# Sums of the later modulations on ScalarE and GpSimd in a two-block transformer kernel

## The chip, the cores and the metric

The kernel runs on one core of one Trainium2 chip. The metric is the device time of one execution in microseconds (us), from the core's first instruction to its last. The core has a TensorE (PE in the profile), a VectorE (DVE), a ScalarE (ACT), a GpSimd (POOL) and a SyncE (SP). SP and POOL issue most of the transfers, ACT some of them.

## The reference

Two blocks of a transformer follow each other: a first block with two layers and a second with one, over 512 tokens of width 2048, all in float32. The part that the change touches is the modulation, a product of one vector with a large matrix, once per layer:

```
c_act = jax.nn.silu(c)
mod = c_act @ w_ada[l] + b_ada[l]          # 2048 x 6144 weights per layer
shift, scale, gate = jnp.split(mod, 3, axis=-1)
h = rms_norm(x, norm_g[l]) * (1.0 + scale[:, None, :]) + shift[:, None, :]
...
x = x + gate[:, None, :] * (... @ w_out[l])
```

Everything else (input products, a state space mixer, differential attention, a gated delta rule, sliding window attention, output products) is the same before and after.

## The kernel before

All five engines walk one list of steps, `plan`. Each engine has a function per kind of step, takes the steps that it has a function for, in the order of the list, and skips the others. So the order of instructions on each engine is fixed when the program is built, and semaphores alone join the engines. TensorE's big products are the main line of the list; other generators are interleaved with it, a step at a time.

The weights of the modulations are 128 rows by 512 columns at a time: `modulation(m)` handles one set of blocks of 512 columns, and for each block it runs over 16 row tiles (`KT`), k = 0 to 15. For each k there is a step `ada_sum` and, one yield later, a step `ada_fetch` for the tile three places on. `ada_fetch` is a transfer that GpSimd issues, into one of three slots (in `side` for m = 1 to 4; two in `gring` and one in `const_two` for m = 5). `ada_sum` adds the row tile, times the silu of c of its 128 rows (one column of `cact`), to an accumulator of 128 x 512 in `tring`. It is one VectorE instruction on line 123 (line 120 for k = 0, which has nothing to add to yet), and it frees the slot. When a block's 16 tiles are summed, TensorE's `ada_turn` multiplies the accumulator with a column of ones, which sums over the 128 partitions and puts the result on partitions. It stands at k = 5 of the next block, and `ada_out` adds the bias later.

The first modulation (shift and scale of the first layer) is done by `first_sum` and `first_row` in the first 150 us and is left alone. The five later ones make 448 sums: 384 with weights in `side`, from 184 to 2355 us, and 64 with weights in `gring` and `const_two`, from 3513 to 3820 us. They are served by `carry()`, which runs `carried[0]` of their steps per step of the main line.

Near them on GpSimd stand the steps `powers`, `angles`, `bc_place` and `lags` of the state space mixer, and `rotate` of the attention, which adds two tiles of `tring` into `q` or `k` (the end of the rotary embedding); VectorE makes both tiles just before. On ScalarE stand copies out of PSUM, the exponentials of the softmax and the state space mixer's copies.

The helpers that record the instructions have one line each: 108 matmul, 111 transpose, 114 activation, 117 tensor_tensor, 120 tensor_scalar, 123 scalar_tensor_tensor, 126 tensor_copy, 132 reciprocal, 138 reduce_max, 147 dma_start. So the profile's rows are told apart by their tiles.

Of the kernel before, what the change touches and what calls it, by code (L numbers as in the profile page):

```python
# [18 lines left out]
KT = D // P  # L19
# [242 lines left out]
def build(nc, d, out, at, ncols):  # L262
    ctx = ExitStack()
    with ctx:
# [3 lines left out]
        def sem(name, owner=None):  # L268
            s = Signal(ctx.enter_context(nc.semaphore(name)), owner)
            signals.append(s)  # L270
            return s
# [144 lines left out]
        wide_clear = sem("wide_c_cleared", pool)  # L416
        a_step = sem("act_step", act)
        x_ready_a = sem("x_ready_by_act", act)
# [213 lines left out]
        def ada_slots(m):  # L632
            return wide_slots if m == GATE_OF[2] else mslots
# [782 lines left out]
        def ada_landed(m, n0, k):  # L1416
            return (late_ada_in if m == GATE_OF[2] else ada_in)[ada_slots(m).where["ada", m, n0, k]]
# [28 lines left out]
        def tensor():  # L1446
# [80 lines left out]
            def ada_turn(m, n0):  # L1527
                acc, bank = temps.at("acc", m, n0), aux.at("mod", m)
                if n0 == mods[m][1][0] * D:
                    room(aux.clear("mod", m))  # L1530
                pe.wait_ge(*ada_ready.of("sum", m, n0))
                for j in range(4):
                    c = n0 // P + j
                    i = pe.matmul(bank[:, c:c + 1], acc[:, j * P:(j + 1) * P], ones[:, 0:1], start=True, stop=True)
                i.then_inc(*ada_turned.up(m, n0))
                temps.leave(("acc", m, n0), pe.mine())
# [368 lines left out]
        def vector():  # L1905
# [150 lines left out]

            def ada_sum(m, n0, k):
                acc, wv, c = temps.at("acc", m, n0), ada_slots(m).at("ada", m, n0, k)[:, 0, :], cact[:, mods[m][0] // 2, k:k + 1]
                dve.wait_ge(*ada_landed(m, n0, k).of("ada", m, n0, k))
                if k == 0:  # L2060
                    room(temps.clear("acc", m, n0))
                    i = dve.tensor_scalar(acc, wv, c, None, M)
                else:
                    own()
                    i = dve.scalar_tensor_tensor(acc, wv, c, acc, M, AD)
                i.then_inc(*(ada_ready.up("sum", m, n0) if k == KT - 1 else d_step.up()))
                ada_slots(m).leave(("ada", m, n0, k), dve.mine())
# [668 lines left out]
            def o_turn(j, k0):  # L2736
                if j % 2 == 0:
# [7 lines left out]
                         norm_roots=norm_roots, final_root=final_root, norm_scale=norm_scale, norm_final=norm_final, prm_turn=prm_turn, rope=rope, ada_sum=ada_sum, ada_out=ada_out, norm_square=norm_square, norm_root=norm_root,  # L2745
# [16 lines left out]
        def scalar():  # L2762
# [41 lines left out]
            def late_fetch():  # L2804
# [14 lines left out]
                par(relb[0:32, :], d["rel_bias_2"])  # L2819

# [372 lines left out]
            steps = dict(save_v2=save_v2, set_by=set_by_, rope=rope, norm_square=norm_square, norm_root=norm_root, x_store=x_store, norm_shift=norm_shift, norm_roots=norm_roots, final_root=final_root,  # L3193
# [13 lines left out]
        def gpsimd():  # L3207
# [8 lines left out]
            def ada_fetch(m, n0, k):  # L3216
                w = d["w_ada_2"][0] if mods[m][0] == 2 else d["w_ada"][mods[m][0]]
                room(passed("delta" if m == GATE_OF[2] else "start"))
                room(ada_slots(m).clear("ada", m, n0, k))
                pool.dma_start(ada_slots(m).at("ada", m, n0, k)[:, 0, :], w[k * P:(k + 1) * P, n0:n0 + 512]).then_inc(  # L3220
                    *ada_landed(m, n0, k).landing("ada", m, n0, k))

# [133 lines left out]
            steps = dict(vec_fetch=vec_fetch, ada_fetch=ada_fetch, powers=powers, angles=angles, bc_place=bc_place, lags=lags, rotate=rotate, band=band_,  # L3356
# [129 lines left out]
```

## Time and profile before

| | before |
|---|---|
| time, median of 3 runs | 4302.54 us (4299.52 to 4306.98) |
| the profiled execution: span | 4304.2 us |
| PE busy | 4128.5 us, 96% |
| DVE busy | 2440.3 us, 57% |
| ACT busy | 807.5 us, 19% |
| POOL busy | 498.5 us, 12% |
| chain that ended last: PE, DVE, ACT, DMA | 82%, 12%, 2%, 2% |

The profiled execution's own time is its span, 4304.2 us; the program lays nothing around it that the profile shows. It is 1.7 us over the median of the three runs. Busy time is the time in which an engine runs an instruction. The chain that ended last is followed back from the last instruction, at each step to what released it.

### The profile page before, as it was taken

To read this page: it belongs to the slowest core of one execution; us is meant where nothing else is said; L and a number is where in the kernel's file an instruction comes from. 1 tells how busy PE (TensorE), PEld (TensorE's weight loads), DVE (VectorE), ACT (ScalarE), POOL (GpSimd) and SP (SyncE) were. 2 spreads that over 40 slices of the span, in tenths; PEclk is the share of its full clock that TensorE was granted. 3 is DMA by queue.
4 is the path that set the end of the run, shared out by engine and by line. 5 is a ranking of instruction groups with operands and counts; after the bars stand their busy time and mean duration, and the time that the engine had idled before them with its cause. 6 is when DMAs were issued, how large, how long until landed. Compare 5 with 4: busy or idle time off the path is not lost.

```text
span 4304.2 us, 41305 instructions
## 1 busy us (share of the span) xinstructions
PE 4128.5 (96%) x16042; PEld 2766.0 (64%) x16042; DVE 2440.3 (57%) x4211; ACT 807.5 (19%) x1450; POOL 498.5 (12%) x816
## 2 busy tenths in 40 slices
PE   6899999999999999999999999999999999999999
PEld 3565544444447555444468568878788877787888
DVE  6576436674533564366666466465655367666643
ACT  2222201131011221011311122121211122230000
POOL 0233111111202231111111000000000101100000
PEclk7999999999999999999999999999999999999999
DMA  9633333334552333332444332222121333434433
GB/s 311 204 118 105 108 122 108 121 124 146 151 166 73 105 113 115 121 121 93 130 142 152 113 102 70 64 69 64 61 73 59 92 104 115 126 98 137 137 103 103
DMA packets 370192, 499.29 MB, mean 116 GB/s; under 512 B 44379, under 2 KB 279118, under 8 KB 369486
## 3 DMA queue, kind: packets, MB, share of 16 engines
q1 hardware_dynamic: 289984, 340.16, 24.5%
q0 software_dynamic: 38608, 125.86, 9.2%
q10 hardware_dynamic: 41406, 30.63, 2.2%
q8 instruction: 127, 2.08, 0.2%
q14 instruction: 67, 0.55, 0.0%
HBM read 462.51 MB, written 34.08 MB: 115 GB/s over the span
## 4 chain that ended last, share of the span: by engine, by line
PE 82%; DVE 12%; ACT 2%; DMA 2%; issue 1%; ACTq 0%; POOL 0%; DVEq 0%; SPq 0%
PE bank L108 80%; DVE tring L132 2%; DVE tring L117 2%; PE bank L111 2%; DVE tring L123 2%; DMA side<-in_w_ada 1%; ACT tring L114 1%; DVE wring L117 1%; DVE dring L120 1%; DVE bank L117 1%; DVE tring L120 1%; DVE dring L117 0%; ACT L114 0%; DVE region_b L117 0%; DVE sring L138 0%
## 5 line engine op out<-in xcount | busy, mean ns | idle before, releaser
L108 PE MATMUL bank<-region_b,wring 128*128 128x256 f32 (+2 forms) x4448 | 1322.8, 451 | 7.8 <-ACT region_b L114 6.6
L108 PE MATMUL bank<-region_a,wring 128*128 128x256 f32 (+1 forms) x3232 | 1083.5, 489 | 29.1 <-DVE wring L117 29.1
L108 PEld LDWEIGHTS bank<-region_b,wring 128*128 128x128 f32 (+1 forms) x4448 | 830.2, 190 | 412.5 <-issue 332.3
L108 PEld LDWEIGHTS bank<-region_a,wring 128*128 128x128 f32 x3232 | 613.8, 194 | 416.2 <-issue 337.8
L147 POOL DMA_DIRECT2D side<-in_w_ada x384 | 209.0, 545 | 1309.9 <-DVE tring L123 951.7
L123 DVE SCALAR_TENSOR_TENSOR tring<-side,cact,tring 128x512 f32<-128x512 f32 x360 | 303.2, 842 | 78.1 <-DMA side<-in_w_ada 42.3
L108 PE MATMUL bank<-wring,region_b 128*128 128x512 f32 (+1 forms) x640 | 265.5, 572 | 10.7 <-ACT region_b L114 10.7
L114 ACT ACT_TABLE_LOAD x160 | 205.3, 1283 | 354.2 <-DVE sring L120 283.8
L117 DVE TENSOR_TENSOR tring<-bank,tring 128x256 f32<-128x256 f32 (+1 forms) x229 | 101.0, 441 | 299.6 <-PE bank L108 296.2
L117 DVE TENSOR_TENSOR wring<-wring 128x1024 f32<-128x1024 f32 (+1 forms) x213 | 234.8, 1102 | 17.4 <-PE bank L108 8.5
L108 PE MATMUL bank<-wring,region_a 128*128 128x512 f32 x512 | 226.8, 601 | 6.0 <-ACT region_a L114 6.0
L114 ACT ACTIVATE tring<-bank 128x512 f32<-128x512 f32 (+1 forms) x166 | 81.4, 493 | 796.5 <-PE bank L108 476.2
L108 PEld LDWEIGHTS bank<-wring,region_b 128*128 128x128 f32 x640 | 150.4, 239 | 118.8 <-issue 89.9
L117 DVE TENSOR_TENSOR tring<-bank,side 32x512 f32<-32x512 f32 (+1 forms) x160 | 110.0, 687 | 163.5 <-PE bank L108 159.5
L108 PEld LDWEIGHTS bank<-wring,region_a 128*128 128x128 f32 x512 | 126.6, 250 | 98.1 <-issue 68.7
L132 DVE RECIPROCAL tring<-tring 128x512 f32<-128x512 f32 x54 | 180.7, 3346 | 15.0 <-ACT tring L114 15.0
L108 PE MATMUL bank<-yaT,wring 128*128 128x512 f32 (+1 forms) x512 | 170.6, 486 | 0.0
L117 DVE TENSOR_TENSOR bank<-bank,tring 128x256 f32<-128x256 f32 (+1 forms) x213 | 110.2, 517 | 84.2 <-PE bank L108 81.7
L117 DVE TENSOR_TENSOR tring<-tring 128x512 f32<-128x512 f32 (+2 forms) x142 | 98.7, 695 | 81.6 <-ACT tring L114 77.2
L108 PEld LDWEIGHTS bank<-yaT,wring 128*128 128x128 f32 x512 | 97.1, 190 | 66.9 <-issue 60.3
L114 ACT ACTIVATE tring<-bank,sring 128x128 f32<-128x128 f32 (+3 forms) x128 | 67.2, 526 | 386.7 <-DVE sring L120 386.5
L111 PE MATMUL bank<-const,tring 128*128 128x128 f32 (+1 forms) x474 | 78.8, 282 | 42.9 <-DVE tring L120 13.0
(285 smaller groups left out, 4320.6 us busy)
## 6 DMA issues: line engine op xcount, KB each, us to landing
wring<-in_w_in SPq DMA_DIRECT2D x180, 1024.0 KB, 5.3
side<-in_w_ada POOLq DMA_DIRECT2D x384, 256.0 KB, 3.2
wring<-in_w_out SPq DMA_DIRECT2D x48, 1024.0 KB, 8.2
yaT<-in_w_ada SPq DMA_DIRECT2D x16, 1024.0 KB, 9.4
wring<-in_w_glu SPq DMA_DIRECT2D x16, 1024.0 KB, 7.7
tring<-x_saved SPq DMA_DIRECT2D x48, 256.0 KB, 2.9
gring<-in_w_ada POOLq DMA_DIRECT2D x43, 256.0 KB, 3.0
SS<-in_w_ada SPq DMA_DIRECT2D x8, 1024.0 KB, 9.8
```

Source lines behind the costliest of these rows:

```text
L108: return self.e.matmul(*a, **k) if self.e else self
L111: return self.e.transpose(*a) if self.e else self
L114: return self.e.activation(*a, **k) if self.e else self
L117: return self.e.tensor_tensor(*a) if self.e else self
L120: return self.e.tensor_scalar(*a) if self.e else self
L123: return self.e.scalar_tensor_tensor(out=o, in0=a, scalar=s, in1=b, op0=op0, op1=op1) if self.e else self
L132: return self.e.reciprocal(*a) if self.e else self
L147: return self.e.dma_start(dst, src, allow_slow_non_contiguous=True) if self.e else self
```

## The change

`ada_sum` leaves VectorE. ScalarE waits for the landing of the tile and scales it by the column of `cact` with a Copy activation, in place in its slot (for k = 0 straight into the accumulator, which frees the slot). GpSimd waits for that, and adds the slot to the accumulator with a tensor_tensor (for k = 1 to 15), which frees the slot. TensorE's `ada_turn` now waits for the last addition. The list of steps is the same.

```diff
@@ tensor, ada_turn
-                pe.wait_ge(*ada_ready.of("sum", m, n0))
+                pe.wait_ge(*rows_added.of(m, n0, KT - 1))
@@ vector
-            def ada_sum(m, n0, k):
-                acc, wv, c = temps.at("acc", m, n0), ada_slots(m).at("ada", m, n0, k)[:, 0, :], cact[:, mods[m][0] // 2, k:k + 1]
-                dve.wait_ge(*ada_landed(m, n0, k).of("ada", m, n0, k))
-                if k == 0:
-                    room(temps.clear("acc", m, n0))
-                    i = dve.tensor_scalar(acc, wv, c, None, M)
-                else:
-                    own()
-                    i = dve.scalar_tensor_tensor(acc, wv, c, acc, M, AD)
-                i.then_inc(*(ada_ready.up("sum", m, n0) if k == KT - 1 else d_step.up()))
-                ada_slots(m).leave(("ada", m, n0, k), dve.mine())
@@ scalar
+            def ada_sum(m, n0, k):
+                w = ada_slots(m).at("ada", m, n0, k)[:, 0, :]
+                act.wait_ge(*ada_landed(m, n0, k).of("ada", m, n0, k))
+                if k == 0:
+                    room(temps.clear("acc", m, n0))
+                act.activation(w if k else temps.at("acc", m, n0), w, ACT.Copy, scale=cact[:, mods[m][0] // 2, k:k + 1]).then_inc(
+                    *rows_scaled.up(m, n0, k))
+                if k == 0:
+                    ada_slots(m).leave(("ada", m, n0, k), act.mine())
@@ gpsimd
+            def ada_sum(m, n0, k):
+                if k == 0:
+                    return
+                acc = temps.at("acc", m, n0)
+                pool.wait_ge(*rows_scaled.of(m, n0, k))
+                own()
+                pool.tensor_tensor(acc, acc, ada_slots(m).at("ada", m, n0, k)[:, 0, :], AD).then_inc(*rows_added.up(m, n0, k))
+                ada_slots(m).leave(("ada", m, n0, k), pool.mine())
```

The order of TensorE's and SyncE's instructions is the same in both programs. On VectorE rows go away and none moves against another. These are the rows where VectorE goes from the rotary embedding of a head (`tring<-bank,side`) to the softmax of the one before (`sring`, `tring<-tring,sring,small`), in the first attention:

```order
 L138 TENSOR_REDUCE sring<-bank 128x1
 L120 TENSOR_SCALAR sring<-sring 128x1
-L123 SCALAR_TENSOR_TENSOR tring<-side,cact,tring 128x512 x3
 L117 TENSOR_TENSOR tring<-bank,side 128x512
 L117 TENSOR_TENSOR tring<-bank,side 32x512 x4
```

Three sums that stood ahead of a head's rotary products are gone, and the same holds ahead of the reciprocals of the softmax.

GpSimd in the same place, from the last step of the first state space mixer to the first two `rotate`, before:

```order
164 L117 TENSOR_TENSOR Tm<-const,prm 128x512
165 L147 DMA side<-in_w_ada 128x512 x5
166 L117 TENSOR_TENSOR q<-tring 128x512
167 L147 DMA side<-in_w_ada 128x512 x3
168 L117 TENSOR_TENSOR q<-tring 128x512
169 L147 DMA side<-in_w_ada 128x512 x4
170 L117 TENSOR_TENSOR k<-tring 128x512
```

and now:

```order
236 L147 DMA side<-in_w_ada 128x512
237 L117 TENSOR_TENSOR tring<-tring,side 128x512
238 L117 TENSOR_TENSOR q<-tring 128x512
239 L147 DMA side<-in_w_ada 128x512
240 L117 TENSOR_TENSOR tring<-tring,side 128x512
241 L147 DMA side<-in_w_ada 128x512
242 L117 TENSOR_TENSOR tring<-tring,side 128x512
243 L147 DMA side<-in_w_ada 128x512
244 L117 TENSOR_TENSOR tring<-tring,side 128x512
245 L117 TENSOR_TENSOR q<-tring 128x512
```

Each fetch has an addition ahead of it, and a `rotate` stands with an addition before it and another, after one fetch, behind it.

ScalarE a little later, between the exponentials of the softmax (`tring,sring<-bank,sring`) and the copies of its transposed weights (`wT<-bank`), before:

```order
234 L114 ACTIVATE tring,sring<-bank,sring 128x128 x2
235 L114 ACTIVATE wT<-bank 128x4x128
236 L114 ACTIVATE tring,sring<-bank,sring 128x256 x2
237 L114 ACTIVATE tring<-tring 128x512
238 L114 ACTIVATE wT<-bank 128x128
```

and now:

```order
300 L114 ACTIVATE tring,sring<-bank,sring 128x128 x2
301 L114 ACTIVATE side<-side,cact 128x512
302 L114 ACTIVATE wT<-bank 128x4x128
303 L114 ACTIVATE side<-side,cact 128x512
304 L114 ACTIVATE tring,sring<-bank,sring 128x256 x2
305 L114 ACTIVATE tring<-tring 128x512
306 L114 ACTIVATE side<-side,cact 128x512
307 L114 ACTIVATE wT<-bank 128x128
```

A scaling, with its wait for a landing, stands between the exponentials and the copies. The loads of activation tables (160) are as many as before and none is added.

## Rows read from the trace of the kernel before

**Rows 1.** Busy time by stretches in which modulations are summed, and their sum

```profile
core 0: us, PE busy (x) PEld busy (x) DVE busy (x) ACT busy (x) POOL busy (x), PEclk, DMA share, GB/s
...
1680.00:2100.00 420.00, 408.74 (x1086) 182.96 (x1085) 229.11 (x429) 68.01 (x149) 61.93 (x93) 0.99 0.34 110
...
sum 2516.00, PE 2453.61 PEld 1391.77 DVE 1449.87 ACT 529.73 POOL 446.00; mean PE 350.51 PEld 198.82 DVE 207.12 ACT 75.68 POOL 63.71
```

**Rows 2.** TensorE's waits from 174 to 2360: total us, times, longest

```profile
PE bank L111 <- DVE tring L123: 12.6, 11, 2.3
PE bank L108 <- ACT tring L114: 11.0, 5, 2.8
PE bank L108 <- ACT region_a L114: 6.0, 1, 6.0
...
PE bank L108 <- POOL k L117: 2.6, 2, 1.3
```

**Rows 3.** Pieces of the chain that ended last: start, length, what

```profile
904.41 1.79 DVE tring L123
...
906.38 0.42 DVE tring L120
...
915.75 0.76 DVE tring L123
...
916.60 0.75 DVE tring L123
...
925.50 0.75 DVE tring L123
...
927.00 0.76 DVE tring L123
...
3771.18 0.76 DVE tring L123
```

**Rows 4.** VectorE's sums: duration in ns, min/median/max, first and last start

```profile
L123 DVE SCALAR_TENSOR_TENSOR tring<-side,cact,tring x360: 750/752/1846, 188.5 to 2353.8; 128x512 f32<-128x512 f32 x180
...
L123 DVE SCALAR_TENSOR_TENSOR tring<-gring,cact,tring x40: 750/752/753, 3516.0 to 3818.4; 128x512 f32<-128x512 f32 x40
```

**Rows 5.** The tile `side`: its users, and who waited for its landings

```profile
L120 DVE TENSOR_SCALAR tring<-side,cact x24: 459/481/750, 184.3 to 2296.4; 128x512 f32<-128x512 f32 x24
...
  DVE tring L123: 42.3, 23
```

**Rows 6.** Timeline from 784 to 800: start, us, instruction, idle before it

```profile
788.87 3.56 DVE L117 TENSOR_TENSOR tring<-bank,side 128x512 f32<-128x512 f32 x5 [3.64 <-PE bank L108]
792.52 1.26 POOL L117 TENSOR_TENSOR q<-tring 128x512 f32<-128x512 f32 x1 [7.31 <-DVE tring L117]
792.54 1.79 DVE L123 SCALAR_TENSOR_TENSOR tring<-side,cact,tring 128x512 f32<-128x512 f32 x1
...
794.50 0.35 DVE L120 TENSOR_SCALAR tring<-tring,sring,small 128x128 f32<-128x128 f32 x1
```

**Rows 7.** Timeline from 349 to 352: VectorE reads PSUM beside GpSimd

```profile
349.02 2.31 DVE L123 SCALAR_TENSOR_TENSOR Tm<-bank,const_one,Tm 128x512 f32<-128x512 f32 x4 [1.25 <-PE bank L108]
349.34 0.30 POOL L117 TENSOR_TENSOR W<-cf,Bn 128x64 f32<-128x64 f32 x1
```

**Rows 8.** GpSimd's operations on line 117: duration in ns, min/median/max

```profile
L117 POOL TENSOR_TENSOR q<-tring x16: 1256/1259/1803, 533.8 to 2044.1; 128x512 f32<-128x512 f32 x16
```

**Rows 9.** GpSimd's fetches into `side`: durations, and time to landing

```profile
L147 POOL DMA_DIRECT2D side<-in_w_ada x384: 537/537/804, 174.3 to 2346.9; - x192
...
DMA to landing us min/median/max: 2.8/3.2/8.4
```

**Rows 10.** ScalarE's groups by form: busy us, mean ns, idle before

```profile
L114 ACT ACTIVATE tring<-tring 128x512 f32<-128x512 f32 x91 | 55.4, 626 | 254.9 <-DVE tring L120 189.6 <-DVE tring L123 46.3 <-DVE tring L126 18.1
...
L114 ACT ACTIVATE tring<-region_a,vec 128x512 f32<-128x512 f32 x16 | 11.3, 707 | 0.0
```

**Rows 11.** GpSimd's waits over the whole span: total us, times, longest

```profile
POOL side L147 <- DVE tring L123: 951.7, 239, 64.9
```

More of the change, by code:

```diff
@@ L416, in build @@
         wide_clear = sem("wide_c_cleared", pool)
+        rows_added = sem("ada_rows_added", pool)
         a_step = sem("act_step", act)
+        rows_scaled = sem("ada_rows_scaled", act)
         x_ready_a = sem("x_ready_by_act", act)
@@ L2744, in vector @@
             steps = dict(vec_turn=vec_turn, w_sum=w_sum, fold=fold, quarter_sums=quarter_sums, quarter_rest=quarter_rest, quarter_last=quarter_last, x_turn=x_turn, first_sum=first_sum, first_out=first_out, sum_square=sum_square,
-                         norm_roots=norm_roots, final_root=final_root, norm_scale=norm_scale, norm_final=norm_final, prm_turn=prm_turn, rope=rope, ada_sum=ada_sum, ada_out=ada_out, norm_square=norm_square, norm_root=norm_root,
+                         norm_roots=norm_roots, final_root=final_root, norm_scale=norm_scale, norm_final=norm_final, prm_turn=prm_turn, rope=rope, ada_out=ada_out, norm_square=norm_square, norm_root=norm_root,
                          keep_u=keep_u, c_turn=c_turn, ssm_params=ssm_params, c_power=c_power,
@@ L3191, in o_turn @@
                     aux.leave(("o_turn", j, k0), act.mine())
-            steps = dict(save_v2=save_v2, set_by=set_by_, rope=rope, norm_square=norm_square, norm_root=norm_root, x_store=x_store, norm_shift=norm_shift, norm_roots=norm_roots, final_root=final_root,
+            steps = dict(ada_sum=ada_sum, save_v2=save_v2, set_by=set_by_, rope=rope, norm_square=norm_square, norm_root=norm_root, x_store=x_store, norm_shift=norm_shift, norm_roots=norm_roots, final_root=final_root,
                          vec_fetch=vec_fetch, vec_turn=vec_turn, x_turn=x_turn, first_keep=first_keep, sum_square=sum_square,
@@ L3354, in band_fetch @@
                         *band_in.landing())
-            steps = dict(vec_fetch=vec_fetch, ada_fetch=ada_fetch, powers=powers, angles=angles, bc_place=bc_place, lags=lags, rotate=rotate, band=band_,
+            steps = dict(vec_fetch=vec_fetch, ada_fetch=ada_fetch, ada_sum=ada_sum, powers=powers, angles=angles, bc_place=bc_place, lags=lags, rotate=rotate, band=band_,
                          d_qd=d_qd, oa_store=oa_store, oa_fetch=oa_fetch, v_fetch=v_fetch, band_fetch=band_fetch, fence=fence_of(pool))
```

## The prediction

> **What bounds the kernel now.** I read the page's busy shares first: PE 96%, DVE 57%, ACT 19%, POOL 12%. TensorE is the bound, so a lighter VectorE is worth only what TensorE idles for it. Next I read the stretches in which modulations are summed (174 to 2360 and 3500 to 3830) [rows 1]: 2516 us in all, of which TensorE is busy 2453.6. So it idles 62.4 us there, 2.5%, and no arrangement of the sums can give more than that. VectorE is busy 1449.9 of those 2516 us, ScalarE 529.7, GpSimd 446.0: there is room on both new engines. Then TensorE's own waits [rows 2]: 12.6 us for an operation of VectorE's line 123, 11.0 for ScalarE (exponentials that come after VectorE), 2.6 for GpSimd's `rotate` into `k`. A single 6.0 is the norm of the second layer, which no sum stands in; the rest is spread thin.
>
> Last I walked the chain that ended last for sums of the later modulations. There are 39 pieces, the first at 792.54, the last at 3771.18, 30.4 us together [rows 3, 6]. Most are 0.75 long, five are 1.78 to 1.84 [rows 3, 4]. In the first state space mixer (174 to 500) there is none.
>
> **What is removed.** 420 fused operations at 0.752 us median, 0.842 mean where `side` is the source, and 28 scalings at 0.48 [rows 4, 5]: about 303 + 45 + 13 = 361 us of VectorE. Off the path that is worth nothing. On the path I set each TensorE wait against the sums on the chain just ahead of it, and took the smaller of the two, since TensorE cannot gain more than it waits. Over some two dozen waits this makes 20.9 us. (At 927.90, for one, TensorE had waited 0.66 us, and the chain has 0.76 + 0.75 + 0.75 of sums before it [rows 3], so 0.66 count.)
>
> **The long sums.** The sum at 792.54 took 1.79 us, not 0.75, and ended when GpSimd's `rotate` (792.52, 1.26 us) was through plus one normal duration [rows 6]. The row shows that a VectorE operation with both tiles in SBUF stands still while GpSimd reads SBUF. At 349.02 four VectorE operations that read PSUM took 2.31 us together beside GpSimd's 128x64 products, their normal time [rows 7]. The reverse is seen too: `rotate` took 1.80 at most, 1.26 in the median [rows 8]. The Trainium skill has it so in "SBUF — State Buffer", Who interferes with whom: VectorE with two SBUF inputs, or in its two-port fast mode, and GpSimd exclude each other for a whole instruction, whoever came first; the trace agrees with its 1.79 against 0.75.
>
> So about 1.04 us of each of the long sums is the price of the `rotate` beside it. That `rotate` stays. With the sum gone, the next VectorE operation that needs the port is the scaling at 794.50 (0.35 us, SBUF to SBUF), which will start behind it instead. All five of the long sums stand ahead of a TensorE wait that is longer than they are; I take 5 x 1.04 = 5.2 us back, and 15.7 us remain.
>
> **What is added on GpSimd.** 420 additions of 128x512 from two SBUF tiles. The same operation is `rotate`: 1.26 us [rows 8]. That is 529 us, and it holds the shared access 529 of 2516 us, 21% of the time. Cost on the chain, from one piece of it (904.4 to 927.8): there ten VectorE pieces need the port (the first at 906.38, the last at 927.00 [rows 3]; the reciprocals, reductions and operations on PSUM don't), 6.2 us together. One addition starts per 6.0 us, so one falls into these ten and holds up what follows by 1.26; and each of the ten finds the port taken with chance 0.21, for 0.63 on average, which is 1.3. That makes 2.6 us of delay where 4.05 us of sums leave (1.79 + 0.76 + 0.75 + 0.75 [rows 3]): 0.63 of what is removed. Over the chain that is 0.63 x 30.4 = 19 us, and with the same share reaching TensorE as above (20.9 of 30.4) it is 13 us. Bounds: 0 if the additions fall where VectorE reads PSUM or idles, and 26 if each meets twice as much. I take 13, since an addition comes when ScalarE has passed the same place in the list, often right beside VectorE's work of that place. The skill's "Perfetto Trace Analysis", Optimizing Scalar/DVE Operations, warns that moving work between VectorE and GpSimd "might not help" because of this port. By that the gain would be nil; the rows leave 15.7 - 13 = 2.7 us.
>
> **What is added on ScalarE.** 448 scalings. The nearest rows are a plain 128x512 at 0.626 and one with a per-partition operand at 0.707 [rows 10]. I take 0.70: 314 us, ScalarE from 19% to 26% busy. It has PSUM copies and exponentials in the same order, and TensorE waits for it in five places, 11.0 us [rows 2]. In some of these a scaling stands just ahead: five at 0.7, less than half of them late, 1 us. VectorE's waits for landings (42.3 us, 23 times [rows 5]) become ScalarE's. I take these at nothing: no TensorE wait of before stood behind them on VectorE, and GpSimd now starts a fetch when ScalarE has passed, not when VectorE has, which is earlier in most places. If that cover is gone they cost up to 42.
>
> **The ring of three slots.** A slot goes round in 0.70 + 1.26 + 0.54 + 3.2 = 5.7 us [rows 8, 9, 10], before in 0.75 + 0.54 + 3.2 = 4.5. Three slots give one tile per 1.9 us; the list asks for one in 5.7 us on average (384 from 174.3 to 2346.9 [rows 9]). So the sums keep pace, and `ada_turn`, some ten yields after the last sum, waits for nothing.
>
> **GpSimd's queue.** Before, it slept on VectorE: 951.7 us for the sums alone [rows 11]. Now a `rotate` can find an addition running ahead of it. It costs where TensorE waits for the `rotate` (2 waits, 2.6 us [rows 2]) and at some near misses: 1 us. `powers`, `angles` and `lags` get later too, but in the mixers TensorE takes their products a round of the mixer later, and I see no wait that they would reach.
>
> **Sum.** -20.9 + 5.2 + 13 + 1 + 1 = -0.7 us. Against the profiled execution's 4304.2, outside which nothing lies, this is 4303.5; the median of the runs is 1.7 lower, so the predicted time is 4301.8 us. About 0.2%, 8.6 us, is what a measurement of this kernel can tell from no change.
>
> **The rivals.**
> Faster: the additions fall beside work that doesn't need the port. Attention speaks for it: there most of VectorE's time is products from PSUM such as the five at 788.87 [rows 6]. Then 15.7 to 20.9 less small change is gained: 4284 to 4289 us.
>
> Slower by the port: additions meet the chain more often. The sum turns to +8.6 when they cost TensorE 22 instead of 13, that is 32 us on the chain, or 25 whole holds of 1.26 among the 420. It speaks for it that an addition follows a `rotate` after one fetch, so that VectorE can find the port held for 2.5 us on end at the very places where TensorE waits [rows 6]. At twice my price it gives +12: 4315 us.
>
> Slower by ScalarE: a landing is late because GpSimd stands in `rotate` or `angles` waiting for VectorE, as it waited 7.3 us at 792.52 [rows 6], ScalarE stands at its scaling, and copies out of PSUM and exponentials behind it wait, which TensorE needs. If a third of the 42.3 us reaches TensorE it is +14: 4316 us. Against it: ScalarE idles four fifths of the time.
>
> No change at all in the waits is not possible: the sums do leave VectorE.
>
> **How the numbers follow.** My forecast, a change within 8.6 us either way, 0.42; faster by the port staying clear, 0.28; slower by the port, 0.18; slower by ScalarE or GpSimd's queue, 0.12. So faster 0.28, same 0.42, slower 0.30. Range 4286 to 4319 us: the lower end leaves out the last of the faster case, the upper covers each slower case alone, not both together. The forecast's own range is 4294 to 4311.
>
> **What would show it.** VectorE's busy time falls by less than the 361 us, to about 2150 to 2250, because its SBUF operations get longer: the 128x1024 and 128x512 ones on `wring` and `tring` should show means well over their minima. GpSimd's additions show a minimum of 1.26 and a mean above it. ScalarE rises to about 1120. TensorE's idle in the seven stretches stays near 62 us, with the entries for line 123 smaller and new ones for VectorE's lines 117 and 120 or ScalarE. The port is priced wrongly if VectorE's other operations keep their durations; ScalarE is, if its waits for landings come before new TensorE waits; and I am wrong altogether if idle falls below 50 or rises above 75.

## The result and the profile after

| | before | after |
|---|---|---|
| median, 20 runs each | 4302.69 us (4298.85 to 4306.98) | 4309.15 us (4303.69 to 4318.14) |
| ratio | 1 | 1.0015, 95% interval 1.0009 to 1.0022 |
| TensorE's idle time in the seven stretches | 62.4 us | 69.5 us |

The changed kernel is 6.5 us slower. That is within what I had called no change (8.6 us either way), and within the range, but on the other side of zero from the predicted time of 4301.8, and the interval excludes that time. (An execution's own time is 1.8 us above its span, 4312.3 against 4310.5 here; the text ahead of the prediction had put the two as equal. The predicted time was counted from the median, so it doesn't hang on that.)

The page of the changed kernel, its busy times, its chain and two of its groups:

```profile
PE 4127.9 (96%) x16042; PEld 2767.0 (64%) x16042; DVE 2265.5 (53%) x3763; ACT 1090.7 (25%) x1898; POOL 1066.0 (25%) x1236
PE 82%; DVE 12%; ACT 2%; DMA 2%; issue 1%; ACTq 0%; POOL 0%; DVEq 0%; SPq 0%; POOLq 0%
L117 POOL TENSOR_TENSOR tring<-tring,side 128x512 f32<-128x512 f32 x360 | 468.0, 1300 | 790.9 <-ACT side L114 781.4
L114 ACT ACTIVATE side<-side,cact 128x512 f32<-128x512 f32 x360 | 250.5, 714 | 188.5 <-DMA side<-in_w_ada 178.9
```

An addition takes 1.30 us, a scaling 0.714: both were costed right (1.26 and 0.70). VectorE's busy time fell by 175 us (2440.3 to 2265.5), not by the 361 us that the sums had taken. The other 186 us are its remaining operations getting longer (26 of them come without any addition: e2 below has 2104.9 us over its whole span, where 361 less would be 2079), and the chain still has 12% of VectorE in it, as before.

The same seven stretches as in [rows 1], their sum, and then TensorE's waits as in [rows 2], from 174 to 2360 us:

```profile
sum 2516.00, PE 2446.50 PEld 1383.42 DVE 1266.19 ACT 806.25 POOL 1011.57; mean PE 349.50 PEld 197.63 DVE 180.88 ACT 115.18 POOL 144.51
```

```profile
PE bank L108 <- ACT tring L114: 11.3, 5, 2.8
PE bank L111 <- DVE tring L123: 9.9, 9, 2.3
...
PE bank L108 <- DMA wring<-in_w_glu: 2.0, 1, 2.0
PE bank L108 <- DVE outT L117: 2.0, 1, 2.0
PE bank L108 <- DVE Tm L123: 1.7, 1, 1.7
```

The wait for line 123 fell from 12.6 us in 11 waits to 9.9 in 9. What it gave went into small waits elsewhere. The last one is new, and so is that for the weights of `in_w_glu`.

**Where it is lost, in three places.** First the place of [rows 6], the timeline of the changed kernel from 784 to 797, of VectorE and GpSimd:

```profile
785.31 3.56 DVE L117 TENSOR_TENSOR tring<-bank,side 128x512 f32<-128x512 f32 x5 [6.29 <-PE bank L108]
...
788.95 1.26 POOL L117 TENSOR_TENSOR q<-tring 128x512 f32<-128x512 f32 x1 [3.11 <-DVE tring L117]
789.17 1.14 DVE L120 TENSOR_SCALAR tring<-tring,sring,small 128x128 f32<-128x128 f32 x1
790.16 0.56 POOL L147 DMA_DIRECT2D side<-in_w_ada  x1
790.34 1.84 DVE L123 SCALAR_TENSOR_TENSOR tring<-tring,sring 128x128 f32<-128x128 f32 x1
790.74 1.28 POOL L117 TENSOR_TENSOR tring<-tring,side 128x512 f32<-128x512 f32 x1
...
795.34 2.08 PE L108 MATMUL bank<-tring,ones 128*128 128x512 f32 x2 [2.75 <-ACT tring L114]
```

The sum of 1.79 us is gone, but the scaling on line 120 now takes 1.14 instead of the 0.35 of [rows 6], because it stands beside `rotate`, and the operation behind it, on line 123, takes 1.84 instead of 0.35, because it meets the addition that follows after one fetch. So -1.79 + 0.79 + 1.49 = +0.49, and TensorE's wait here grew from 2.23 to 2.75 us. Its row before was:

```profile
798.38 1.12 PE L108 MATMUL bank<-tring,ones 128*128 128x512 f32 x2 [2.23 <-ACT tring L114]
```

The wait had a second price. The granted clock around it, in the changed kernel (the eighth column is PEclk):

```profile
792.00:794.00 2.00, 0.59 (x3) 0.14 (x1) 1.83 (x8) 0.56 (x2) 0.57 (x2) 1.00 0.36 107
794.00:796.00 2.00, 0.66 (x1) 0.50 (x2) 1.75 (x6) 1.91 (x5) 0.01 (x1) 0.73 0.25 98
796.00:798.00 2.00, 2.00 (x3) 0.67 (x2) 0.00 (x0) 1.89 (x3) 1.70 (x2) 0.50 0.00 0
798.00:800.00 2.00, 2.00 (x6) 0.98 (x5) 0.00 (x0) 0.75 (x2) 1.25 (x2) 0.92 0.40 131
```

TensorE had idled from 792.6 to 795.3. In this time the clock fell from 1.00 to 0.50 (from 2.4 to 1.2 GHz), and it stayed there until after 798; the two products at 795.34 took 2.08 us instead of 1.12. The length of a wait alone doesn't tell when this happens. In the kernel before, the clock stayed at 1.00 through a wait of 2.83 us (before the product at 2027.37) and fell to 0.50 behind one of 2.41 (851.52) and one of 2.06 (1349.19). So this place shows what a fall costs, and not that half a microsecond more of waiting brings one.

The second place is in the output products. The timeline from 2216 to 2223:

```profile
2216.62 2.20 POOL L117 TENSOR_TENSOR tring<-tring,side 128x512 f32<-128x512 f32 x1 [4.46 <-ACT side L114]
2217.72 4.86 DVE L117 TENSOR_TENSOR outT<-yaT,outT 128x1024 f32<-128x1024 f32 x2
...
2220.22 1.27 POOL L117 TENSOR_TENSOR tring<-tring,side 128x512 f32<-128x512 f32 x1
```

The same two VectorE operations, and TensorE's wait for them, before:

```profile
2220.14 2.49 DVE L117 TENSOR_TENSOR outT<-yaT,outT 128x1024 f32<-128x1024 f32 x2
...
2222.68 1.99 PE L108 MATMUL bank<-outT,wring 128*128 128x256 f32 x8 [0.50 <-DVE outT L117]
```

Together they lost 2.37 us, nearly two whole additions, and TensorE's wait for `outT` grew from 0.50 to 2.02 us. Before, the chain has one sum ahead of them here, 0.76 us at 2214.44, and the wait was 0.50: half a microsecond to gain, and 1.52 lost.

The third place is a queue, in the first mixer, 490 to 500:

```profile
493.26 0.72 ACT L114 ACTIVATE side<-side,cact 128x512 f32<-128x512 f32 x1 [0.40 <-ACT tring L114]
...
494.07 1.26 POOL L117 TENSOR_TENSOR tring<-tring,side 128x512 f32<-128x512 f32 x1 [6.16 <-ACT side L114]
495.47 1.04 POOL L117 TENSOR_TENSOR Tm<-const,prm 128x512 f32<-128x512 f32 x1
...
496.61 2.31 DVE L123 SCALAR_TENSOR_TENSOR Tm<-bank,const_one,Tm 128x512 f32<-128x512 f32 x4 [5.39 <-POOL Tm L117]
```

GpSimd waits for ScalarE's scaling, `Tm` stands behind that addition in GpSimd's queue, VectorE waits 5.4 us for `Tm`, and TensorE waits 1.69 us for VectorE where it waited for nothing. In the window attention (3500 to 3830) TensorE's waits for line 120 grew too, from 12.4 us to 16.2.

The wait for `in_w_glu` (2.04 us at 2091.04) is not a late issue. SyncE issues the load 1.87 us ahead of the same product of TensorE in both kernels (2086.47 and 2088.34 before, 2083.11 and 2084.98 now). Now TensorE can use it only 7.93 us after the issue; before, it used it after 5.73 us without a wait. So it is the transfer that took longer; what slowed it is open.

### The profile page after: what moved, and what is told of

It is laid out like the page before. It is cut to its first block, busy times and chain, and to the rows that moved or that the text cites. A ratio compares the mean times of both kernels' runs of the same rounds, so it can differ in the third digit from the quotient of the medians.

```text
span 4310.5 us, 41445 instructions
## 1 busy us (share of the span) xinstructions
PE 4127.9 (96%) x16042; PEld 2767.0 (64%) x16042; DVE 2265.5 (53%) x3763; ACT 1090.7 (25%) x1898; POOL 1066.0 (25%) x1236
## 3 DMA queue, kind: packets, MB, share of 16 engines
q8 instruction: 127, 2.08, 0.2%
## 4 chain that ended last, share of the span: by engine, by line
PE 82%; DVE 12%; ACT 2%; DMA 2%; issue 1%; ACTq 0%; POOL 0%; DVEq 0%; SPq 0%; POOLq 0%
PE bank L108 80%; DVE tring L117 2%; DVE tring L132 2%; PE bank L111 2%; DMA side<-in_w_ada 1%; DVE tring L123 1%; DVE wring L117 1%; ACT tring L114 1%; DVE tring L120 1%; DVE dring L120 1%; DVE bank L117 1%; DVE dring L117 0%; ACT L114 0%; DVE s_delta L117 0%; DVE region_a L123 0%
## 5 line engine op out<-in xcount | busy, mean ns | idle before, releaser
L117 POOL TENSOR_TENSOR tring<-tring,side 128x512 f32<-128x512 f32 x360 | 468.0, 1300 | 790.9 <-ACT side L114 781.4
L114 ACT ACTIVATE side<-side,cact 128x512 f32<-128x512 f32 x360 | 250.5, 714 | 188.5 <-DMA side<-in_w_ada 178.9
L117 DVE TENSOR_TENSOR wring<-wring 128x1024 f32<-128x1024 f32 (+1 forms) x213 | 254.6, 1195 | 19.7 <-PE bank L108 9.2
L117 DVE TENSOR_TENSOR tring<-tring 128x512 f32<-128x512 f32 (+2 forms) x142 | 111.9, 788 | 88.2 <-ACT tring L114 83.4
```

The lines of the kernel that those rows point to most:

```text
L114: return self.e.activation(*a, **k) if self.e else self
L117: return self.e.tensor_tensor(*a) if self.e else self
```

## The experiments

Ratios are against the kernel before on the same chip, with 95% intervals. Idle is that of TensorE in the seven stretches (2516 less the sum of PE), in one profiled execution each. "VectorE" is its busy time there. The profiled executions already differ at the start, where the change touches next to nothing: one copy of VectorE into `region_a` starts at 189.14 us before, at 180.50 in the changed kernel and at 184.09 in e4, which is the changed kernel again. So spans of single executions aren't compared; idle repeats better (69.5 and 69.8).

| run | ratio | idle | VectorE |
|---|---|---|---|
| e1 no sums | 0.9947 (0.9934 to 0.9959) | 48.8 | 1131.8 |
| e2 scalings only | 0.9938 (0.9925 to 0.9950) | 47.5 | 1123.6 |
| e3 GpSimd only writes | 0.9950 (0.9937 to 0.9964) | 51.1 | 1141.6 |
| e4 the change again | 1.0014 (1.0005 to 1.0023) | 69.8 | 1271.0 |
| e5 change in attention only | 0.9996 (0.9987 to 1.0005) | 62.1 | 1375.8 |
| e6 in the other products only | 1.0009 (1.0001 to 1.0018) | 64.9 | 1414.4 |
| e7 in the window attention only | 1.0004 (0.9996 to 1.0013) | 65.8 | 1437.7 |
| e11 in the mixers only | 0.9997 (0.9988 to 1.0006) | 63.4 | 1387.5 |
| e8 before, sums one place ahead | 0.9964 (0.9951 to 0.9978) | 53.5 | 1448.1 |
| e12 the same at two places | 0.9963 (0.9951 to 0.9976) | 53.2 | 1450.6 |
| e9 changed, additions one place ahead | 0.9980 (0.9972 to 0.9989) | 62.6 | 1275.8 |
| e10 GpSimd adds without ScalarE | 1.0079 (1.0066 to 1.0092) | 85.2 | 1299.3 |
| e13 the same at ScalarE's pace | 1.0011 (1.0003 to 1.0020) | 66.7 | 1272.1 |
| e14 e10, GpSimd only writes | 0.9952 (0.9938 to 0.9965) | 51.8 | 1145.7 |

**e1, e2, e3, e4: the change taken apart.** e1 leaves the 420 sums out altogether. On ScalarE only k = 0 is done. GpSimd waits for each landing itself and writes one column in place of an addition:

```diff
@@ scalar, ada_sum
+                if k:
+                    return
@@ gpsimd, ada_sum
-                pool.wait_ge(*rows_scaled.of(m, n0, k))
+                pool.wait_ge(*rows_scaled.of(m, n0, 0))
+                pool.wait_ge(*ada_landed(m, n0, k).of("ada", m, n0, k))
...
-                pool.tensor_tensor(acc, acc, ada_slots(m).at("ada", m, n0, k)[:, 0, :], AD).then_inc(*rows_added.up(m, n0, k))
+                pool.memset(acc[:, 0:1], 1.0).then_inc(*rows_added.up(m, n0, k))
```

> The changed kernel without 15 of 16 scalings and without the additions: ScalarE scales only k = 0 of each block, and GpSimd waits for each landing and writes one column of the accumulator (about 0.1 us) in place of adding. So neither VectorE, ScalarE nor GpSimd works on the sums, and GpSimd reads nothing for them. The prediction's first term, 20.9 us off before (15.7 if rotate's hold goes over to the next VectorE operation): ratio 0.9951 to 0.9964. If the sums on VectorE's chain were worth nothing because another wait ends just behind them, it stays within 3 us of before.

e2 keeps ScalarE's scalings and lets GpSimd return at once, so that ScalarE frees the slots and TensorE's `ada_turn` waits for the last scaling:

> The changed kernel without the additions: ScalarE scales every tile and frees the slot, GpSimd only fetches. Port theory: within 2 us of the kernel without any sums, some 15 us under before. ScalarE theory (scalings and their waits for landings hold up copies and exponentials): 6 us or more above the kernel without sums.

e3 keeps the scalings and gives GpSimd two memsets of the accumulator in place of each addition, together nearly as long (1.13 us against 1.28), which read nothing. The sums are left out, as in e1 and e2:

```diff
@@ gpsimd, ada_sum
-                pool.tensor_tensor(acc, acc, ada_slots(m).at("ada", m, n0, k)[:, 0, :], AD).then_inc(*rows_added.up(m, n0, k))
+                pool.memset(acc, 1.0).then_inc(*g_step.up())
+                own()
+                pool.memset(acc, 1.0).then_inc(*rows_added.up(m, n0, k))
```

> The changed kernel with each addition on GpSimd replaced by two memsets of the accumulator (about 1.1 us together), so GpSimd's queue is as long, the waits are the same, and GpSimd reads no SBUF for the sums; the sums are left out. Port theory: VectorE's operations with two SBUF inputs keep their normal durations, and most of the difference to the kernel with scalings alone is gone; those in its fast mode may still wait if writing is enough to exclude them. Queue theory (rotate, Tm and the fetches behind additions): the time is that of the changed kernel, about 1.0015.

e4 is the changed kernel once more, beside them on the same chip:

> The changed kernel once more, as the measure for the other three on this chip: 1.0015, and a TensorE idle of about 69 us in the stretches with sums. If its waits at 499 and 2091 us (Tm behind an addition; a weight load that came late) are there again they belong to the change; if not they are chance. The 7 us by which its first 174 us were shorter than before's should not be there again.

The sums of the stretches, of e2, e3 and e4 in this order:

```profile
sum 2516.00, PE 2468.49 PEld 1409.97 DVE 1123.64 ACT 809.88 POOL 438.22; mean PE 352.64 PEld 201.42 DVE 160.52 ACT 115.70 POOL 62.60
```

```profile
sum 2516.00, PE 2464.88 PEld 1406.14 DVE 1141.59 ACT 809.32 POOL 893.08; mean PE 352.13 PEld 200.88 DVE 163.08 ACT 115.62 POOL 127.58
```

```profile
sum 2516.00, PE 2446.17 PEld 1385.26 DVE 1271.00 ACT 812.56 POOL 1010.83; mean PE 349.45 PEld 197.89 DVE 181.57 ACT 116.08 POOL 144.40
```

Read by the column PE: idle is 62.4 before, 47.5 without the sums but with all scalings (-14.9), 51.1 with GpSimd busy 455 us more but reading nothing (+3.6), and 69.8 when GpSimd reads (+18.7). By the column DVE the same VectorE work takes 1141.6 beside memsets and 1271.0 beside additions: 129 us more. In time, by the ratios: -26.7, then +5.2, then +27.5, in sum +6.0 us. The steps are larger in time than in idle. Most of the rest is TensorE's busy time: the same 16042 products were busy for 4128.5 us before, 4113.1 in e2, 4116.4 in e3 and 4122.7 in e4, over the whole span. From e3 to e4 that is 19.9 us of idle and 6.3 of busy time, 26.2 together, close to the 27.5 by the ratios. The clock is where busy time can grow, as the windows around 796 showed, and the mean granted clock over all runs goes with it: 0.9819 before (0.980 in the profiled execution, which is on the low side), 0.9842 in e2, 0.9834 in e3, 0.9821 in e4. But the busy time of two executions of the changed kernel differs by 5.2 us (4127.9 and 4122.7), so only the first of these steps is clear of the scatter.

ScalarE had 178.9 us of waits for landings in the changed kernel. e2 has all its scalings, and is no slower than e1, which has none of them: they cost nothing that can be measured.

The place at 789 in e3, timeline:

```profile
789.18 1.14 DVE L120 TENSOR_SCALAR tring<-tring,sring,small 128x128 f32<-128x128 f32 x1
...
790.35 0.35 DVE L123 SCALAR_TENSOR_TENSOR tring<-tring,sring 128x128 f32<-128x128 f32 x1
790.73 1.13 POOL L129 MEMSET tring<- 128x512 f32 x2
...
793.87 1.13 PE L108 MATMUL bank<-tring,ones 128*128 128x512 f32 x2 [1.26 <-ACT tring L114]
```

`rotate` still holds up the scaling (1.14), although that operation has one tile in SBUF as its input and not two. The next operation has its 0.35 back, and TensorE waits 1.26 us instead of 2.75: 1.49 less, which is 1.84 - 0.35 to the hundredth. So the addition behind `rotate` alone makes the difference between a gain of 0.97 us and a loss of 0.52 at this wait. (The two memsets are 0.15 us shorter than the addition and leave off once in between. That small a difference in GpSimd's queue isn't likely to make 18.7 us, but e3 doesn't exclude that it makes a part.) The Trainium skill ("SBUF — State Buffer", Who interferes with whom) says that a VectorE instruction with two SBUF inputs contends with a GpSimd instruction that reads SBUF, and not with one that only writes it. The trace agrees: e3's 1141.6 us are near e2's 1123.6, and the operation at 790.35 keeps its 0.35 us.

**e5, e6, e7, e11: the change in one part at a time.** The set of sums that move is a condition, and all others stay on VectorE: 160 in the first five blocks of the second and fourth modulation (they fall in the attention), 96 in their last three, 64 in the fifth modulation, and 128 in the first and third (in the mixers).

```diff
+        def moved(m, n0):
+            i = (n0 - mods[m][1][0] * D) // 512
+            return m in (2, 4) and i < 5
```

> The new scheme only for the 10 blocks of 512 columns that are summed during the two attentions (m = 2 and 4, first five blocks), VectorE's fused sum for the other 18. Port theory with a rotate, then an addition on end: what leaves VectorE in the chain (about 13 us of long and short sums) comes back as longer SBUF operations of the softmax, so within 3 us of before. If the additions fell beside PSUM work as my faster rival had it: 8 to 12 us less than before.

> The new scheme only for the 6 blocks summed during the output products of the layers (m = 2 and 4, last three blocks). In the changed kernel TensorE waited 1.5 us more for outT and 1.2 us more for wring there, where 128x1024 sums of VectorE stood still beside additions. Port theory: 2 to 5 us above before. Otherwise within 2 us.

> The new scheme only for the last modulation (m = 5), beside the sliding window attention. In the changed kernel TensorE waited 3.3 us more there, at the scalings of the probabilities (L120, SBUF to SBUF, 1.67 us for two in place of 0.62 beside an addition). Port theory: 3 to 5 us above before. If that was chance: within 2 us.

> The new scheme only for the 8 blocks summed during the state space mixers (m = 1 and 3). Port theory: TensorE hardly waits for VectorE there, so little is gained and little lost; with the new wait for Tm at 499 us (1.7) against the one at 1428 that shrank (1.8): within 3 us of before. The four parts of the change should add up to the whole, +6: attention -2, products +4, window +2, so mixers about +2.

They give -1.7, +3.9, +1.7 and -1.3 us, +2.6 together, each uncertain by about 4. So in time I can't tell the parts apart, nor their sum from the whole of +6.0. e7 falls below the 3 to 5 us that the port theory expected. By idle they are told apart better: -0.3, +2.5, +3.4 and +1.0, which is +6.6 against +7.1 and +7.4 of the whole. In e7 TensorE's waits for line 120 in the window attention are the changed kernel's, 16.2 us. No part hides a gain of 15 us that another eats up. In the attention, where most of the gain was expected, e5 shows next to none: the price is paid in the same place.

**e8, e12, e9: where in the list the sums stand.** In the attention VectorE's sums stand between the rotary products (`use` of the projection, line 117) and the softmax, on the way to TensorE. `carry()`, which serves a step of the modulations, is called one line earlier, so that VectorE sums while it waits for TensorE's projection. e8 does this to the kernel before, e9 to the changed kernel:

```diff
@@ dense
+                carry()
                 do(job.use, jid, j, *job.args)
                 banks.give(jid, j)
                 follow(after(j) if after else None)
-                carry()
                 yield
```

> The kernel before with one line moved in dense(): carry(), which puts the sums of the modulations into the list, stands ahead of a product's use instead of behind it. So VectorE's sums come while it still waits for TensorE, and not between the rotary products and the softmax that TensorE waits for. If the sums on the chain are what costs the 15 to 20 us, half or more of it is gained: 0.9965 to 0.998. Rival: the softmax stands behind rotate and then meets the port, and the sum now delays the rotary products themselves where VectorE was not idle: within 3 us of before.

> The changed kernel with carry() ahead of a product's use in dense(), so that scalings and additions stand ahead of the rotary products in the list, where VectorE waits for TensorE, and no addition stands directly behind a rotate ahead of the softmax. Port theory: an addition that falls into VectorE's idle time costs nothing, so the waits after the rotary products shrink as in the kernel before with the same line moved, and the time is well under before: 0.996 to 0.998. Rival (it is the mere number of additions that counts, not where they fall): 1.001 to 1.002 minus a few us, about before.

e8 is, with e12, the fastest kernel that computes the reference: 4283.88 us, 15.5 less than before by the ratio and 22 less than changed. Its sum of the stretches, and its wait at 791:

```profile
sum 2516.00, PE 2462.52 PEld 1403.26 DVE 1448.06 ACT 528.19 POOL 441.85; mean PE 351.79 PEld 200.47 DVE 206.87 ACT 75.46 POOL 63.12
```

```profile
786.52 1.26 POOL L117 TENSOR_TENSOR q<-tring 128x512 f32<-128x512 f32 x1 [7.44 <-DVE tring L117]
786.73 1.14 DVE L120 TENSOR_SCALAR tring<-tring,sring,small 128x128 f32<-128x128 f32 x1
...
787.90 0.35 DVE L123 SCALAR_TENSOR_TENSOR tring<-tring,sring 128x128 f32<-128x128 f32 x1
...
791.40 1.12 PE L108 MATMUL bank<-tring,ones 128*128 128x512 f32 x2 [1.24 <-ACT tring L114]
```

VectorE is as busy as before (1448.1 against 1449.9), and idle of TensorE is down by 8.9 us to 53.5. The wait is 1.24 us, as in the kernel where GpSimd only writes. Nothing was moved to another engine; the sums merely stand where VectorE had idled. (`carry()` serves the fetches and `ada_turn` too, so these stand earlier as well; e8 doesn't part them from the sums.) The same call moved in the other loop over projections too adds nothing (e12), where 1 to 3 us were expected:

> The kernel before with carry() ahead of the use in fast() too, which serves the last modulation beside the sliding window. Its sums then stand ahead of the kept products instead of ahead of the softmax of the window. If TensorE's waits there (12.4 us for line 120) contain the sums ahead of them (about 3 us), it gains 1 to 3 us over moving the line in dense() alone (0.9964). Rival: in fast() other work of VectorE fills that place and the sum delays it instead: no gain, or 1 to 2 us lost.

e9 shows the other half. In the changed kernel the additions now run during VectorE's idle time, and its timeline has four of them ahead of `rotate`, at 780.81, 782.96, 785.11 and 787.27, and the next only at 795.94, when TensorE has gone on. From the last of them on:

```profile
786.75 3.56 DVE L117 TENSOR_TENSOR tring<-bank,side 128x512 f32<-128x512 f32 x5 [7.17 <-PE bank L108]
787.27 1.28 POOL L117 TENSOR_TENSOR tring<-tring,side 128x512 f32<-128x512 f32 x1
...
790.39 1.26 POOL L117 TENSOR_TENSOR q<-tring 128x512 f32<-128x512 f32 x1 [1.84 <-DVE tring L117]
790.60 1.13 DVE L120 TENSOR_SCALAR tring<-tring,sring,small 128x128 f32<-128x128 f32 x1
...
791.77 0.35 DVE L123 SCALAR_TENSOR_TENSOR tring<-tring,sring 128x128 f32<-128x128 f32 x1
```

(The addition at 787.27 falls beside the five products from PSUM, which keep their 3.56 us.) The wait is 1.26 us again, and the kernel is 8.6 us faster than before and some 15 faster than changed. It doesn't reach e8, since the waits that have nothing to do with this place stay, those for line 120 in the window attention (16.2 us, 12.0 in e8) and these:

```profile
PE bank L108 <- DMA wring<-in_w_glu: 3.4, 1, 3.4
...
PE bank L108 <- DVE outT L117: 2.0, 1, 2.0
```

**e10, e13, e14: a surprise, and what it was.** In e10 GpSimd waits for each landing itself and adds the tile unscaled; ScalarE does only k = 0. The product with `cact` is left out for the other rows.

```diff
@@ scalar, ada_sum
+                if k:
+                    return
@@ gpsimd, ada_sum
-                pool.wait_ge(*rows_scaled.of(m, n0, k))
+                pool.wait_ge(*rows_scaled.of(m, n0, 0))
+                pool.wait_ge(*ada_landed(m, n0, k).of("ada", m, n0, k))
```

> The changed kernel without ScalarE's scalings for k over 0 (they are left out): GpSimd waits for the landing itself and adds the unscaled tile. ScalarE theory: 5 us or more under the changed kernel. Port theory: the time of the changed kernel, 1.000 to 1.002.

It took 4337.88 us, 34 us over the kernel before, with the same 420 additions and less other work. Every theory of mine missed that. The timeline from 1432 to 1447, in the second layer's mixer:

```profile
1431.95 0.58 POOL L147 DMA_DIRECT2D side<-in_w_ada  x1
1432.39 1.80 DVE L117 TENSOR_TENSOR CA<-pw,CT 128x320 f32<-128x320 f32 x1
1432.55 1.28 POOL L117 TENSOR_TENSOR tring<-tring,side 128x512 f32<-128x512 f32 x1
1434.13 0.56 POOL L147 DMA_DIRECT2D side<-in_w_ada  x1 [0.30 <-POOL tring L117]
1434.23 0.49 DVE L117 TENSOR_TENSOR tb<-pw,CT 128x320 f32<-128x320 f32 x1
1434.71 1.28 POOL L117 TENSOR_TENSOR tring<-tring,side 128x512 f32<-128x512 f32 x1
1434.76 1.60 DVE L123 SCALAR_TENSOR_TENSOR CA<-CA,tb 128x320 f32<-128x320 f32 x1
...
1436.46 3.17 DVE L120 TENSOR_SCALAR tring<-tring 128x512 f32<-128x512 f32 x2
```

GpSimd had stood for 8.3 us at an operation that waited for VectorE. When it came free, it ran the additions that it was owed one behind the other, fetch and addition, without a wait for a landing, just as VectorE worked through the same stretch. The product on the second row takes 1.80 us where the one on the fifth, beside a fetch, takes 0.49; the two scalings at 1436.46 take 3.17 us together, and 0.43 each undisturbed. TensorE waits 5.36 us at 1446.16. In the changed kernel ScalarE hands out the additions. It stands in the list behind its copies out of TensorE's banks and its exponentials, and I took it that this keeps them apart.

That was a reading of one place, so two more kernels put it to the test. In e13 ScalarE again waits for every landing and releases each addition, but scales only one column of the tile. e14 is e10 with the two memsets of e3 for each addition.

```diff
@@ e13: scalar, ada_sum
-                act.activation(w if k else temps.at("acc", m, n0), w, ACT.Copy, scale=cact[:, mods[m][0] // 2, k:k + 1]).then_inc(
+                out = w[:, 0:1] if k else temps.at("acc", m, n0)
+                act.activation(out, w[:, 0:1] if k else w, ACT.Copy, scale=cact[:, mods[m][0] // 2, k:k + 1]).then_inc(
                     *rows_scaled.up(m, n0, k))
```

> ScalarE waits for each landing as in the changed kernel but scales one column of the tile only (all of it for k = 0), and GpSimd adds the otherwise unscaled tile once ScalarE has done that: the additions keep ScalarE's pace, and ScalarE's load is gone. Theory pace (adding without ScalarE lost 34 us because GpSimd, which then waits for landings itself, ran its additions in trains of two to four with fetches between them): ratio 1.000 to 1.003 against the kernel before, idle of TensorE in the seven stretches 65 to 72 us. Theory timing by chance (any shift of the additions by a microsecond costs or gains tens of microseconds): anything from 0.995 to 1.010, idle far from 69.5. Rival scaling (the full scaling held ScalarE's exponentials up and costs something that the scale-only run hid): 0.999 or less, idle 60 to 64.

> As the kernel in which GpSimd waits for the landings itself and adds unscaled tiles, but with two memsets of the accumulator in place of each addition, so GpSimd's queue and pace are nearly the same and it reads nothing. Theory trains at the port (VectorE waits for the reads of a train): ratio 0.994 to 0.998, idle 50 to 58 us. Rival queue (the 34 us come from GpSimd's own queue: sums and rotates late behind waits, landings late): 1.003 to 1.008, idle 70 to 85, and the waits near 194, 959 and 1428 us stay at 3.8 to 5.4 us.

The sums of the stretches of e10 and e14:

```profile
sum 2516.00, PE 2430.80 PEld 1365.83 DVE 1299.26 ACT 537.50 POOL 997.66; mean PE 347.26 PEld 195.12 DVE 185.61 ACT 76.79 POOL 142.52
```

```profile
sum 2516.00, PE 2464.18 PEld 1404.66 DVE 1145.66 ACT 547.70 POOL 884.02; mean PE 352.03 PEld 200.67 DVE 163.67 ACT 78.24 POOL 126.29
```

Both came out as the theory of pace and port has it. With ScalarE's pace back and a third of the scalings' load (ScalarE is busy 912.9 us, against 1090.8 in e4 and 825.0 in e10), e13 is at 1.0011, with the changed kernel. So the load is hardly it, as e2 had shown with the whole load. With the reads taken away, e14 is at 0.9952 with GpSimd's own waits still in it, with e3; the queue is not it either. At ScalarE's pace the reads of 420 additions cost 1.0014 - 0.9950, 27.5 us; at GpSimd's own pace 1.0079 - 0.9952, 55 us. VectorE gets longer by 129 and 154 us, so it seems that it isn't mainly the amount of the delay that doubles but where it falls: TensorE's idle takes 0.14 of it in the one case and 0.22 in the other.

## Why the prediction was off

The forecast was no change, as the outcome of two large opposite terms. That picture holds; the port's term, put at 13 us, was too small. That the error in time is only some 7 us is partly luck: counted in time, what is removed was too small as well, by 7 to 11 us, and the two errors stand against each other.

- **What is removed, -20.9 + 5.2 = -15.7 us: right.** e2 measures -14.9 of idle. In time it is worth 23 to 27 us (e1, e2): TensorE's busy time falls with its idle time, by 15.4 us in e2's profiled execution, or by some 10 as an estimate from the mean clocks of all runs (0.0023 of 4128). The sum counted waits alone, for gains and for losses.
- **The hold of `rotate` passes to the next operation: right.** The scaling went from 0.35 to 1.14 us at the place named.
- **The port, +13 us: the step that failed.** e4 against e3 gives +18.7 of idle and 27.5 in time. The working had put ten VectorE pieces against one addition and a chance of 0.21 each, as if additions fell at random; its last sentence said that they come "often right beside VectorE's work of that place", and then took the value for random ones. They don't fall at random: the list puts one behind `rotate`, where VectorE's short operations for the softmax are. And it counted the port only in proportion to the sums on the chain. At 2217.72 two operations of 128x1024 lost 2.4 us where one sum of 0.76 went. In the window attention, at 3681.02, a pair of scalings of 128x256 took 1.67 us instead of 0.62 where the chain had no sum at all ahead of the wait, which grew from 0.27 to 1.94 us. Of this growth the longer pair makes 1.05 us; the other 0.6 are ScalarE's, whose scaling at 3677.38 (0.71 us) stands ahead of a table load and the exponentials that VectorE waits for. The rival "slower by the port" named this mechanism, gave it 0.18, and set its point of decision at 22 us instead of 13. In idle the measured 18.7 lies between.
- **ScalarE, +1 us: right in sum.** e2 with all scalings is no slower than e1 (idle 47.5 and 48.8), though single waits such as the one at 3682.84 hold some of it. The rival by ScalarE (+14) is refuted by e2.
- **GpSimd's queue, +1 us: too small.** e3 less e2 is +3.6 of idle, and 5 in time, though the intervals of the two overlap. The sentence "I see no wait that they would reach" missed the 1.69 us at 499, where `Tm` stands behind an addition that stands behind a scaling. The wait for `in_w_glu` was not foreseen either; it is in e3, e4, e5 and e9 too (1.4 to 3.4 us), so it isn't chance, nor does it need additions. The load lands later after its issue; why is open.
- **In sum,** with ScalarE inside the first term: -14.9 + 3.6 + 18.7 = +7.4 of idle against -0.7 predicted (e4's 69.8 less 62.4). That +7.4 shows as only 6 us, where the parts of it show as more than themselves, is within the scatter of the ratios (some 4 us).
- **Of the signs named:** VectorE's busy time was to be 2150 to 2250 and is 2265.5; the means over the minima came (128x512 additions on `tring` on VectorE 839 ns, 715 before and 729 beside e3's memsets; those of 128x1024 on `wring` 1342 ns, 1222 in both); idle is 69.5, under the 75 at which I would have been wrong altogether.

The faster rival, that additions fall beside work from PSUM, is true of the five products at 787 in e9, which kept their 3.56 us, but it isn't what happens in most places.

## What to carry to other kernels

Before moving work off an engine that isn't the bound, see whether the same work can stand elsewhere in its own queue: one call moved by three lines gave 15.5 us, where taking the work to two engines that idled over 80% cost 6.5. Where GpSimd gets work that reads SBUF, don't price it as an average share of time: look at each wait of the bound engine for what VectorE does just ahead of it, SBUF to SBUF, and whether the order puts a GpSimd operation there, above all one behind another. What releases the GpSimd work matters as much as its amount.

## What was not expected of the hardware

- GpSimd's memsets of 128x512, 0.53 us each on average, hardly delay VectorE: with 455 us more of them VectorE is 18 us longer busy (e3 against e2), with additions 129 us more (e4 against e3).
- An operation of 0.35 us on VectorE took 1.84 beside a GpSimd addition of 1.28 (790.34 in the changed kernel). It lost more than the addition's own recorded length, and by the records it had begun 0.40 us ahead of the addition, time enough to finish. Whether the addition's record begins late, or the hold begins before it, these rows don't tell.
- The granted clock fell to one half within a wait of 2.75 us, and was still there over 2 us after TensorE had begun again; the two products behind it took 0.96 us more. The waits of 2.23 and 1.26 us at the same place in the kernel before and in e3 had none of it, but elsewhere one of 2.06 did and one of 2.83 didn't.
- The reads of the same 420 additions cost 27 us or 55, by what releases them.
